# A decoder layer in split float32: the gate and up products by a Strassen step of seven block products, then the down projection over 12, 16 and 16 tiles of k

## The reference, cut to what matters

```
gate, up = split(rmsnorm(h, g_ffn) @ w_gate_up)   # h: 520 x 2048, w_gate_up: 2048 x (2 x 5632)
h = h + (silu(gate) * up) @ w_down                # w_down: 5632 x 2048
h = h + sigmoid(rmsnorm(h, g_ple) @ w_ple_gate) * (p_i @ w_ple_proj)
```

## Time and profile before

| what | value |
|---|---|
| median of 3 runs | 2521.62 us (2518.71 to 2521.93) |
| the profiled execution | 2519.99 us, span 2518.2 us |
| granted clock of TensorE, mean | 0.987 of full speed |
| PE busy | 2450.3 us, 97% of the span, 20127 matmuls |
| DVE busy | 1024.7 us, 41% |
| ACT busy | 766.5 us, 30% |
| POOL busy | 192.7 us, 8% |
| DMA | 271.24 MB, mean 108 GB/s |
| feed-forward block, from its first matmul to the last of the down projection | 740.96 to 2262.42 us |

### The profile page before, as it was taken

The page is one execution under the profiler, slowest core; times in us unless marked ns, Lnnn a source line. Parts: engine busy times, 40 slices in busy tenths (PEclk is TensorE's granted clock), DMA queues, the critical chain, the costliest instruction groups (busy, mean ns, idle before and its releaser), DMA issues.

```text
span 2518.2 us, 46363 instructions
## 1 busy us (share of the span) xinstructions
PE 2450.3 (97%) x20127; PEld 2403.5 (95%) x20127; DVE 1024.7 (41%) x1141; ACT 766.5 (30%) x956; POOL 192.7 (8%) x87
## 2 busy tenths in 40 slices
PE   7999999999999999999999999999999999998996
PEld 6989988989999999999999999999999999998996
DVE  5455556563243433333333333333333334335432
ACT  5334444442232121222212221222222221135442
POOL 0031321102220000000000000000000000031111
PEclk8999999999999999999999999999999999999998
DMA  7446544444322323233232323232322332322242
GB/s 248 153 129 195 191 154 151 156 137 119 87 84 84 101 84 100 84 99 84 83 100 86 97 83 100 83 100 83 100 83 85 98 100 84 91 80 76 79 108 68
DMA packets 371320, 271.24 MB, mean 108 GB/s; under 512 B 5153, under 2 KB 336498, under 8 KB 370841
## 3 DMA queue, kind: packets, MB, share of 16 engines
q1 hardware_dynamic: 354137, 257.28, 34.3%
q10 hardware_dynamic: 17112, 12.95, 1.6%
HBM read 257.30 MB, written 13.37 MB: 107 GB/s over the span
## 4 chain that ended last, share of the span: by engine, by line
PE 95%; DVE 2%; ACT 1%; issue 1%; DMA 1%; POOL 0%; SPq 0%; ACTq 0%; DVEq 0%; POOLq 0%
PE acc L535 89%; PE scores L535 2%; PE mail_bank L535 1%; PE o_bank L535 1%; DVE w_low L1452 1%; DMA region<-in_x_prompt 1%; PE mail_bank L697 0%; ACT w_high L1079 0%; PE mail_bank L1044 0%; POOL sums L1933 0%; DVE small L1576 0%; ACT v_now L1135 0%; PE scores L589 0%; PE mail_bank L763 0%; ACT region L1435 0%
## 5 line engine op out<-in xcount | busy, mean ns | idle before, releaser
L535 PE MATMUL acc<-x_high,w_high 128*128 128x260 f32 x4864 | 999.8, 286 | 21.0 <-DVE x_low L1460 12.2
L535 PE MATMUL acc<-x_high,w_low 128*128 128x260 f32 x4864 | 984.9, 284 | 0.0
L535 PE MATMUL acc<-x_low,w_high 128*128 128x260 f32 x4864 | 984.0, 283 | 0.0
L535 PEld LDWEIGHTS acc<-x_high,w_high 128*128 128x128 f32 x4864 | 753.3, 189 | 44.3 <-issue 35.1
L535 PEld LDWEIGHTS acc<-x_high,w_low 128*128 128x128 f32 x4864 | 754.0, 189 | 0.0
L535 PEld LDWEIGHTS acc<-x_low,w_high 128*128 128x128 f32 x4864 | 752.9, 189 | 0.1
L1452 DVE TENSOR_TENSOR w_low<-raw,w_high 128x2048 fp32r<-128x2048 f32 x196 | 449.0, 2291 | 226.9 <-ACT w_high L1079 225.6
L1079 ACT ACTIVATE w_high<-raw 128x2048 fp32r<-128x2048 f32 x196 | 373.9, 1907 | 507.0 <-PE acc L535 500.4
L535 PE MATMUL acc<-act_low,w_high 128*128 128x260 f32 x1408 | 283.2, 283 | 0.0
L535 PE MATMUL acc<-act_high,w_high 128*128 128x260 f32 x1408 | 282.5, 282 | 0.0
L535 PE MATMUL acc<-act_high,w_low 128*128 128x260 f32 x1408 | 281.3, 281 | 0.0
(11 more groups left out here) (223 smaller groups left out, 1109.0 us busy)
## 6 DMA issues: line engine op xcount, KB each, us to landing
raw<-in_w_gate_up SPq DMA_DIRECT2D x88, 1024.0 KB, 5.8
raw<-in_w_down SPq DMA_DIRECT2D x44, 1024.0 KB, 5.2
raw<-in_w_in SPq DMA_DIRECT2D x32, 1024.0 KB, 6.9
key_pages<-in_cache_k SPq DMA_DIRECT2D x32, 512.0 KB, 5.5
region<-in_cache_v SPq DMA_DIRECT2D x32, 512.0 KB, 5.5
raw<-in_w_out SPq DMA_DIRECT2D x16, 1024.0 KB, 5.8
raw<-in_w_ple_gate SPq DMA_DIRECT2D x16, 1024.0 KB, 7.0
h_spill<-region ACTq DMA_DIRECT2D x1, 4160.0 KB, 16.5
```

The source lines that it names most:

```text
L535: return pe.matmul(o, l, r, start=start, stop=stop)
```

## The change

**Strassen step.** The first STD = 3 of the 44 pairs stay as they are. For the other NS = 41, the pair's weights are cut into four blocks: gate or up, by first or second half of k (HK = 8 tiles, HS = 1024 columns each). The input is cut into four as well: half of k by half of the tokens. The step, in Winograd's form, needs seven products of 8 tiles of k by 260 tokens where the plain way has eight. Sums of blocks are made in float32 before the split:

* On the input side, once: ACT scales each row of h, DVE makes four sums of 260 columns of each of 8 pairs of rows (`t_step`). Three of the sums are split into new buffers `xt_h` and `xt_l`; the fourth replaces a quarter of `xh` and `xl` (`t4_highs`, `t4_lows`).
* On the weight side, for each pair: DVE makes four sums of 1024 columns in place in the raw slabs, and seven blocks (A11, S1, S2, A12, S3, S4, A22) are split. The high and low parts have four places of 1024 columns, used in the order 0, 1, 2, 3, 0, 1, 2.
* On the output side, for each pair: three PSUM banks are used, x, y and z (three more for the next pair). ACT copies partial results out four times, DVE joins them in six steps.

Raw weights of the odd pairs go to a new place in `keys`, so two whole pairs are in SBUF.

**Order.** All 44 pairs come first. Each result, split into high and low, is stored to DRAM (two DMAs of 260 KB). The down projection then runs over three groups (`CHUNKS`) of 12, 16 and 16 tiles of k; in each, 16 columns of 128 outputs are computed over all of the group's k tiles, with `add_h` after each: 48 additions. The results are loaded back from DRAM in groups of four tiles (1.04 MB for the high, the same for the low), into the places of `xt_h`, `xh` and their low parts. The down slabs are 128 columns wide instead of 512 and hold 12 or 16 tiles of k. The transposes of the embedding input move behind the fourth column of the down projection.

The core of the diff:

```diff
-CH = 4
-NCH = DFF // P // CH
+FF = DFF // P
+STD = 3
+NS = FF - STD
+CHUNKS = (12, 16, 16)
+PLACE = (0, 1, 2, 3, 0, 1, 2)
...
@@ SyncE
+            def pair_step(n, odd):
+                store_act(n + STD - 1, odd)
+                sp.wait_ge(S["part_low"], 7 * (n + 1))
+                load_pair(n + 2, odd)
...
+            store_act(FF - 3, 1)
+            sp.wait_ge(S["part_low"], 7 * (NS - 1))
+            sp.dma_start(p_nat, p_prompt[0, 0].rearrange("(b p) n -> p b n", p=P)).then_inc(S["p_landed"], 16)
...
+            store_act(FF - 2, 0)
...
+            sp.wait_ge(S["prod_done"], 7 * (NS - 1) + 2)
+            load_xt(0, 1)
+            sp.wait_ge(S["prod_done"], 7 * (NS - 1) + 3)
+            load_xt(4, 2)
+            load_down(0)
+            load_down(1)
+            sp.wait_ge(S["prod_done"], 7 * (NS - 1) + 5)
+            load_xt(8, 0)
+            store_act(FF - 1, 1)
...
@@ TensorE
+            def half_product(s, i, bank, moving, start=False):
+                pe.wait_ge(S["part_low"], 7 * s + i + 1)
...
+                for k in range(HK):
+                    col = slice(at + k * P, at + (k + 1) * P)
+                    add(w_high[:, col], moving[0][:, k, :], k == 0, False)
+                    add(w_high[:, col], moving[1][:, k, :], False, False)
+                    ins = add(w_low[:, col], moving[0][:, k, :], False, k == HK - 1)
+                ins.then_inc(S["prod_done"], 1)
...
+                half_product(s, A11, x, b11, True)
...
+                half_product(s, S1, z, t1, True)
+                pe.wait_ge(S["copied"], 4 * s + 1)
+                half_product(s, S2, x, t2)
+                half_product(s, A12, y, b21, True)
+                pe.wait_ge(S["copied"], 4 * s + 3)
+                half_product(s, S3, x, t3)
+                half_product(s, S4, z, b22)
...
+                pe.wait_ge(S["copied"], 4 * s + 4)
+                half_product(s, A22, x, t4)
...
@@ ScalarE, one window (pair n)
+                part(n, A11, raw11)
+                act.wait_ge(S["sum_done"], 4 * n + 1)
...
+                    act.wait_ge(S["prod_done"], 7 * n - 1)
+                part(n, S1, raw21)
...
+                    act.wait_ge(S["prod_done"], 7 * n)
+                act.wait_ge(S["sum_done"], 4 * n + 2)
+                part(n, S2, raw11)
+                part(n, A12, raw12)
+                if not first:
+                    act.wait_ge(S["joined"], 6 * n - 1)
+                    act.activation(g_row[last], g_row[last], ACT.Silu).then_inc(S["silued"], 1)
+                act.wait_ge(S["prod_done"], 7 * n + 1)
+                act.wait_ge(act_stored[par], 32 * stored)
+                copy(n, g[:, 0:HT], bank_x[1 - par])
...
@@ VectorE, one window (pair n)
+                dve.wait_ge(landed[1], 16 * turns)
+                add_sum(raw21, raw21, raw22, ALU.add)
+                joins(1)
+                part(n, A11, raw11)
+                joins(2)
...
+                add_sum(raw11, raw21, raw11, ALU.subtract)
+                part(n, S1, raw21)
...
+                joins(3, 4)
...
+                add_sum(raw21, raw22, raw11, ALU.subtract)
+                joins(5)
+                part(n, S2, raw11)
+                joins(6)
+                part(n, A12, raw12)
...
+                add_sum(raw12, raw12, raw11, ALU.subtract)
...
+                act_rows(p, last)
+                part(n, S3, raw21)
...
+                act_low(p, last)
+                part(n, S4, raw12)
+                part(n, A22, raw22)
...
@@ VectorE (and ScalarE alike), the first three pairs
+            t_step(0)
+            gate(0)
+            t_step(1)
+            up(0)
+            t_step(2)
+            t_step(3)
+            gate(1)
+            t_step(4)
+            up(1)
+            t_step(5)
+            t_step(6)
+            gate(2)
+            t_step(7)
...
@@ TensorE, first and last of the order
-            pe.wait_ge(S["p_copied"], 1)
+            pe.wait_ge(S["naturals_copied"], 3)
             first_two(Slab(FFN_N), Slab(FFN_N + 1), FFN_T, 1)
...
+            with pe.Fori(0, (NS - 3) // 2) as j:
+                strassen(2 * j + 3, 1)
+                strassen(2 * j + 4, 0)
+            for i in range(4):
+                column(i)
+            turn_p()
```

More of the change, by code:

```diff
@@ L501, in _, with src_ffn @@
                 load(Slab(OUT_N + 1, j), src_out(2 * j + 1))
[L503 to L511, removed]
+            def src_ffn(p, up):
+                return w_gu_v[:, :, ds(up * DFF + p * P, P)]
@@ L968, in _, with pair_of @@
             with pe.Fori(3, KD // 2) as j:
                 out_pair(j)
-            def gate_up(c, j):
+            def pair_of(p):
                 for s in (0, 1):
-                    whole(Slab(FFN_N + s, c * (FFN_STEP // 2) + j), acc[s], FFN_T + s + c * FFN_TSTEP + 2 * j)
-            def down(c, i):
-                for s in (0, 1):
[L980 to L997, removed]
@@ new lines, in down @@
+            def down(slab, i, c, waits):
+                for k in range(CHUNKS[c]):
+                    if waits and k % 4 == 0:
+                        if c == 1:
+                            pe.wait_ge(xh_landed[k // 4], 32)
+                        elif k == 12:
+                            pe.wait_ge(xh_landed[0], 64)
+                        else:
+                            pe.wait_ge(xt_landed[(1, 2, 0)[k // 4]], 32 if c == 0 else 64)
+                    col = slice(k * P, (k + 1) * P)
+                    ins = product(acc[(i + 1) % 2], wh[slab.home][:, col], wl[slab.home][:, col],
+                                  act_tile((xh, xt_h), c, k), act_tile((xl, xt_l), c, k), k == 0, k == CHUNKS[c] - 1)
+                ins.then_inc(S["acc_ready"], 1)
@@ L1388, in wp @@
+            for m in range(KD):
+                if m < KD - 1:
+                    after(DOWN_T + 2 * KD + m, Slab(DOWN_N + 2 * KD + m + 2))
+                act.wait_ge(S["acc_free"], DOWN_T + 2 * KD + m + 1)
+                square(2, m, m % 2)
             def wp(j):
@@ new lines, in _, with column @@
+            for step in range(1, 6):
+                join(NS - 1, step, 1)
+            low(Slab(DOWN_N), CHUNKS[0])
+            join(NS - 1, 6, 1)
+            dve.wait_ge(S["joined"], 6 * NS)
+            act_rows(FF - 1, 1)
+            low(Slab(DOWN_N + 1), CHUNKS[0])
+            dve.wait_ge(S["act_product"], FF)
+            act_low(FF - 1, 1)
+            def column(c, i, half, m, n):
+                add_h(DOWN_T + i + 2 * half, acc[(i + 1) % 2], m)
+                if n:
+                    low(Slab(DOWN_N + i + 2, half), n)
```

530 lines of the change are left out of this document (415 added, 115 removed).

## The result

| | before | after |
|---|---|---|
| median of 4 runs | 2520.16 us (2518.49 to 2521.93) | **2413.03 us** (2411.99 to 2414.68) |
| ratio to before | | 0.9575, 95% interval 0.9559 to 0.9592 |
| the profiled execution, its span | 2519.99, 2518.2 us | 2411.99, 2410.2 us |

A forecast was written before the change was run, and what follows sets the result against it. The prediction took PE's matmuls as the bound in the feed-forward block. 2520.0 - 117.9 + 12.5 + 15.4 - 5 = 2425.0, and 1.6 more for the median gave 2426.6 us, range 2411 to 2447.

The forecast's parts named there:

- 984 matmuls fewer: Feed-forward pairs: 168 matmuls instead of 192 in each of 41 Strassen pairs, at 0.1198 us each, -117.9 us.
- waits in steady windows: Strassen windows after the entry: PE never stalls, since DVE and ACT work fits under 20.13 us; 0.
- entry: Pairs 1 and 2 and the first window: PE waits for half sums and splits, 10.7 us plus clock; +12.5.
- hand-over: Windows to down projection: PE waits for the first slab behind stores and loads, 13 us plus 2.4 clock; +15.4.
- gap behind the block, with the clock: After the feed-forward block: the 8.7 us wait shrinks to 4.2, with less time at half clock; -5.
- One bank: Strassen matmuls: neighbours now stay in one PSUM bank instead of mostly alternating; no change of rate taken.
- Rival 2: Strassen matmuls: 0.017 us more each in the same bank costs 117 us, all that is saved; 2520 to 2540, chance 0.02.
- copy out of bank x: Each window, on ACT: done at 4.65 us, PE needs it at 5.75; margin 1.1, or 2.4 without a table load.
- Rivals 1 and 3: Windows: 1, DVE becomes the bound, +31, chance 0.13; 3, DVE half again as slow, clock falls, +106, chance 0.04.
- Rival 1's chain: Each window, from the fifth product's end: DVE and ACT work through A11 to S2 takes 9.8 of 11.5 us.
- The table load: ACT in the windows: one 1.28 us load per loop turn of two windows, with no drain taken.
- Rival 4: Hand-over to the down projection: queue at 230 GB/s and late result loads, +15, 2442 us; chance 0.08.

## Why the prediction was right, and which terms were off

| term | forecast, us | measured, us |
|---|---|---|
| 984 matmuls fewer | -117.9 | -117.4 (41 x (23.008 - 20.145)) |
| waits in steady windows | 0 | 0 |
| entry | +12.5 (5 to 20) | +4.3 |
| hand-over | +15.4 (9 to 28) | +12.1 |
| gap behind the block, with the clock | -5 (-2 to -7) | -4.8 |
| stages ahead of the block | none | -2.1, scatter of one execution |
| sum | -95.0 | -108.0, with rounding |

- **The bound and the matmuls** were right: PE, with no wait before and none in the windows after. The eighth product put the 118 us back.
- **One bank.** "I take no change of rate" held: 2504 matmuls in 300 us. Rival 2 is out.
- **The windows.** "0" was right. The forecast named S2 as the first to be late, with margins of 1.7 us (S2), 1.1 or 2.4 (copy out of bank x) and 2.9 (A11). Measured: 2.5, 2.3 and 2.9. DVE was 81% busy, not 88%. Rivals 1 and 3 are real mechanisms. Here 2.5 us more vector work a window cost 0.25 us, 3.8 make PE wait in each window for the chain of DVE and ACT, and 5 bring the clock down too. Rival 1's chain was right in kind, but at its end A11 was late by more than S2.
- **The table load** of "half a load a window" does not exist in the changed kernel, whose block has one. The forecast took one for each turn of the loop, beside the 40 of the old one. It cost nothing, since it lay in ACT's idle time.
- **The entry is the term that was mis-sized.** "Low part ready at 793.4", "A11 is ready at 821" and S2's 2.6 us gave waits of 3.5, 4.6 and 2.6, together 10.7; they were 0.39, 1.06 and 1.69, together 3.1. The other 1.2 of the 4.3 us have no wait in the trace: at a granted clock of 1.00 the matmuls between these waits take a little longer (behind the wait of 1.69 us 72 take 8.89 us, later 8.66). The working added durations. The rows after show that neighbours on one engine overlap (DVE's timeline):

```profile
773.09 0.42 DVE L2153 TENSOR_TENSOR key_pages<-key_pages 128x260 f32<-128x260 f32 x1
773.55 0.43 DVE L2155 TENSOR_TENSOR key_pages<-key_pages 128x260 f32<-128x260 f32 x1
...
774.48 0.43 DVE L2159 TENSOR_TENSOR key_pages<-key_pages 128x260 f32<-128x260 f32 x1
774.82 1.10 DVE L2146 TENSOR_TENSOR half_sums_low<-key_pages,half_sums_high 128x260 fp32r<-128x260 f32 x3
```

  The four sums, each waiting for its own engine's last result, stand 0.46 us apart. The forecast had 0.43 and some 0.15 of wait. The three low parts take 1.10 us together, 0.34 from start to start, not 3 x 0.43. A step of seven operations so takes 2.8 us instead of 3.5. The waits then stayed short enough to leave the clock at 1.00, so the two terms of the estimate fell together. That this chain is what sets the waits is shown by the doubled low parts; how much of the 8.2 us between forecast and measurement the overlap explains is not shown.
- **The hand-over** was right in mechanism, and its last step was too high: the working gave 11.3 at 360 GB/s, and 13 was taken. From SP's first store to the slab's landing it was 1628.12 to 1645.45, 17.3 us, where 15.5 + 2 was forecast; but result 42's low part is ready 11.7 us before PE's last product ends, not 9.6. The clock took less than the 2.4 us of the forecast: the first 288 matmuls take 36.10 us where 0.1198 each would be 34.5, so 1.6. A later wait of 0.7 us for a reload had no term, and the last 0.7 of the 12.1 us have no wait in the trace. The Trainium skill, DMA: Bandwidth & Descriptors, section "Anatomy of one DMA", gave an estimate of 14.8 us for the 5.6 MB. Its fit is for single DMAs issued by GpSimd, and here several stood in SP's queue, so the measured 17.3 us do not test it; they bear out the rates in the rows. Rival 4 did not come: no stretch ran as low as its 230 GB/s.
- **The gap behind the block** was right in size: -4.8 for -5, and its length of 4.7 us for 4.2. Its path was not quite the forecast's: the forecast went through ACT's second high part and x_high, the chain goes through DVE's two low parts (1.97 us). The kernel with the later split shows what they cost, 1.3 us.
- **The total.** Entry and hand-over were both taken too dear, by 8.2 and 3.3 us, and the scatter of the stages ahead went the same way, 2.1. No error made up for another. The scatter had no term and left only 2 us to the end of the range; that it did not take more was luck.

## What to carry to other kernels

Count a chain on one engine by the spacing of starts, not by the sum of durations. The trace of the kernel before shows the difference where two operations follow one another (on DVE 2.29 us from 744.45, and the next from 746.66), and the term in which durations were added had most of the error. When matmuls are traded for vector work under a full TensorE, find for each product how much earlier its operands are ready than needed, and keep that above zero in every turn. Waits of 0.95 us in each window cost 1.2, and one of 2.0 us cost 3.6. And a new store and reload through DRAM costs its queue time once: the stores moved behind what PE needs next gained about 4 us, and the slab moved ahead of the reloads no more, since PE then waited for the last of the reloads.

## What the runs showed of the hardware that was not expected

- Waits of 2.0 to 2.2 us, once in each window of 24 us, brought the granted clock to 0.50 for some 3 us each time. The prediction looked for this only behind idle times of over 3 us. Waits of 0.75 to 1.0 us each window left it at 1.00. What lies between was not tried.
- Operations in a row start before the earlier one's recorded end. On DVE 1024 columns are 1.22 us long and 1.14 from start to start, and 260 are 0.42 and 0.34. On ACT a copy of 0.39 us at 1222.50 is followed at 1222.79. The Trainium skill, ScalarE: Activation LUTs, section "What ACT_TABLE_LOAD costs", says that ACTIVATEs in a row overlap by about 93 ns; the 0.10 us here agree. DVE does the same, by 0.08.
- Behind a wait, or where an operand is ready only just in time, the next matmuls took longer at a granted clock of 1.00: 72 in 8.8 to 8.9 us instead of 8.66, in the kernels with two and three more operations and with the table load. What makes them longer was not tried.
- Table loads went from 40 in the block's loop to one in the whole block, though both kernels call the silu once a pair, in loops. Which of the two programs' differences decides it was not tried.
